# Feed-forwards of a two-block transformer kernel: gate and up weights asked for ahead of the down rows, and a chunk's activations turned behind the first block product of the next chunk

## The reference

```python
def swiglu(h, w_gate, w_up, w_down):
    return (jax.nn.silu(h @ w_gate) * (h @ w_up)) @ w_down

for l in range(DEPTH):                       # DEPTH = 2
    ...
    h = rmsnorm_2(x, norm_pre[l, 0]) * (1.0 + sc1) + sh1
    y = swiglu(h, ffn_w_gate[l, 0], ffn_w_up[l, 0], ffn_w_down[l, 0])
    ...
    h = rmsnorm_2(x, norm_pre[l, 2]) * (1.0 + sc3) + sh3
    y = swiglu(h, ffn_w_gate[l, 1], ffn_w_up[l, 1], ffn_w_down[l, 1])
```

## Time and profile before

| | us |
|---|---|
| three runs | 4084.64, 4093.05, 4095.47; median 4093.05 |
| the profiled execution, device time | 4084.79 |
| its span in the trace | 4083.0 (1.8 lie around it) |
| TensorE busy in the span | 3566.2 (87%) |
| VectorE busy | 2672.0 (65%) |
| ScalarE busy | 701.1 (17%) |
| mean granted TensorE clock | 0.941 of full speed |

### The profile page before, as it was taken

How to read it: one execution, slowest core, us unless ns; L and a number is a source line. 1 busy time by engine, 2 the same in 40 slices (tenths; PEclk the granted TensorE clock), 3 DMA queues, 4 the chain that set the end, 5 groups by cost and what they waited for, 6 DMA issues and landing times. The chain is left out here.

```text
span 4083.0 us, 41858 instructions
## 1 busy us (share of the span) xinstructions
PE 3566.2 (87%) x14754; PEld 2593.6 (64%) x14754; DVE 2672.0 (65%) x5286; ACT 701.1 (17%) x1904; POOL 607.6 (15%) x520
## 2 busy tenths in 40 slices
PE   7999986799998889998997767665889999999999
PEld 3678874677777778776784323222667676667676
DVE  2654778978787767766548887776574543574533
ACT  2531111400000000005212111101001301001301
POOL 0000000033232222210004445442000000000000
PEclk9999998999999999999999988767999999999999
DMA  4466545699999999982658999998883345683353
GB/s 173 154 176 199 148 147 209 205 392 416 412 407 375 399 412 417 417 328 89 181 179 356 416 420 388 422 422 319 276 268 123 134 155 168 229 280 129 125 164 114
DMA packets 486873, 1096.66 MB, mean 269 GB/s; under 512 B 21748, under 2 KB 335092, under 8 KB 419862
## 3 DMA queue, kind: packets, MB, share of 16 engines
q1 hardware_dynamic: 375544, 503.78, 36.4%
q0 software_dynamic: 73728, 536.90, 32.0%
q10 hardware_dynamic: 37408, 53.48, 3.9%
HBM read 1078.36 MB, written 15.73 MB: 268 GB/s over the span
## 5 line engine op out<-in xcount | busy, mean ns | idle before, releaser
L1699 PE MATMUL ps<-hT,wring 128*128 128x256 f32 x2048 | 488.4, 393 | 66.7 <-DMA wring<-in_v_tab 54.2
L1699 PEld LDWEIGHTS ps<-hT,wring 128*128 128x128 f32 x2048 | 395.4, 196 | 152.3 <-issue 87.9
L1690 PE MATMUL ps<-hT,wring 128*128 128x256 f32 x2048 | 470.3, 383 | 1.4 <-ACT G L1759 1.1
L1690 PEld LDWEIGHTS ps<-hT,wring 128*128 128x128 f32 x2048 | 382.9, 190 | 78.4 <-DMA wring<-in_u_first 28.2
L2043 PE MATMUL ps<-pairs,diag 128*128 128x512 f32 x520 | 286.8, 712 | 134.7 <-ACT diag L2138 134.7
L1737 POOL DMA_INDIRECT first_pairs<-in_uv_first_rows,eid x171 | 196.5, 1149 | 1152.5 <-POOLq L135 619.3
L2615 PE MATMUL ps<-wring,hff 128*128 128x512 f32 x704 | 309.4, 592 | 1.7 <-ACT hff L2848 1.7
L2043 PEld LDWEIGHTS ps<-pairs,diag 128*128 128x128 f32 x520 | 116.1, 230 | 303.4 <-ACT diag L2138 164.4
L2576 PE MATMUL ps<-wring,hT 128*128 128x256 f32 x1280 | 302.3, 390 | 0.4 <-DVE xT L3039 0.3
L2100 POOL DMA_INDIRECT pairs<-in_uv_second,eid x172 | 206.4, 1200 | 492.0 <-DVE eid L1339 276.9
L2576 PEld LDWEIGHTS ps<-wring,hT 128*128 128x128 f32 x1280 | 248.2, 197 | 36.3 <-DVE xT L3039 2.4
(11 more groups left out here) (413 smaller groups left out, 5285.8 us busy)
## 6 DMA issues: line engine op xcount, KB each, us to landing
wring<-in_u_first SPq DMA_DIRECT2D x128, 512.0 KB, 14.6
wring<-in_v_tab SPq DMA_DIRECT2D x128, 512.0 KB, 11.2
room<-in_ada_w ACTq DMA_DIRECT2D x32, 1536.0 KB, 10.0
wring<-in_ffn_w_gate SPq DMA_DIRECT2D x44, 1024.0 KB, 7.7
wring<-in_ffn_w_up SPq DMA_DIRECT2D x44, 1024.0 KB, 10.8
wring<-in_ffn_w_down SPq DMA_DIRECT2D x44, 1024.0 KB, 5.0
wring<-in_w_in SPq DMA_DIRECT2D x72, 512.0 KB, 6.6
wring<-in_w_mod SPq DMA_DIRECT2D x28, 1024.0 KB, 5.6
```

The source lines that it names most:

```text
L1690: m = nc.tensor.matmul(ps[:, 4 + e % 2, 0:S], uslot[:, e % 3, k, :], hT[:, k, S:2 * S], start=k == 0, stop=k == KD - 1)
L1699: m = nc.tensor.matmul(ps[:, n // 2, (n % 2) * S:(n % 2 + 1) * S], vslot[:, e % 2, n * P:(n + 1) * P], act_[:, e % 3, :], start=e == 0 and ...
```

## The change

SyncE's list: for chunks 2 to 10 the gate and up transfers of a chunk now stand ahead of the down rows of the chunk before it. TensorE's list: `turn_hidden` of chunk j - 1 no longer stands behind the down product of chunk j - 2, but behind the first of the seven block products of chunk j; that first product, which writes bank 4 anew, gets a wait for the first `Silu` of chunk j - 1, which reads bank 4. The last chunk's `turn_hidden` stays behind its down product. VectorE's and ScalarE's lists are as before.

```diff
                 def load_ffn(F):
...
-                    for j in range(NCH):
+
+                    def gate_and_up(j):
                         s = ffn_slot(F, j)
                         if j >= 2:
                             sp.wait_ge(gu.sem, 2 * NCH * F + 2 * (j - 1))
...
+
+                    def down_rows(j):
+                        s = ffn_slot(F, j)
                         if j >= 2:
                             sp.wait_ge(down.sem, (NCH - 1) * F + j - 1)
...
+
+                    for j in range(2):
+                        gate_and_up(j)
+                        down_rows(j)
+                    for j in range(2, NCH):
+                        gate_and_up(j)
+                        if j > 2:
+                            down_rows(j - 1)
+                    down_rows(NCH - 1)
...
                         pe.wait_ge(combd.sem, 4 * (F + 1))
+                    else:
+                        pe.wait_ge(silu.sem, 2 * NCH * F + 2 * j - 1)
                     pe.wait_ge(wgu[s].sem, 32 * nth(F, j))
                     product(4, lambda k: hT[:, k, 0:P], lambda k: low[:, k, :], True).then_inc(prods.sem, 1)
+                    if j > 1:
+                        turn_hidden(F, j - 1)
...
                     for j in range(1, NCH):
                         split_gate_up(F, j)
                         down_(F, j - 1)
-                        turn_hidden(F, j)
+                    turn_hidden(F, NCH - 1)
```

## The result

The changed kernel takes 4034.14 us (median of 4 runs, 4032.63 to 4038.51) against 4092.1 for the kernel before (4 runs, 4084.64 to 4095.47): a ratio of 0.9863, 95% interval 0.9845 to 0.9880, 58 us less. The profiled execution of the changed kernel took 4033.65 us, its span is 4031.9.

The account below looks back on a forecast made before the run. F = 1 and 3 were taken as bound by TensorE, F = 0 and 2 as losing 58.8 us to late weights (39.9 waits, 18.9 lower clock); 4093.05 less 58.8, no cost added, gave 4034 us, range 4019 to 4060.

Parts of the forecast that it names:

- the 58.8 us of the stages: Chunks 2 to 9 of F = 0 and 2: their loss against F = 1 and 3, 58.8 us, about all to win.
- The moved ask: SyncE: gate and up of the next chunk asked for at T - 6.8 in place of T + 0.2.
- The landing: Gate and up weights: 16.5 us after the ask, 18.0 for a slow one; assumed to land before T + 8.
- T + 8: T is the start of a chunk's first product; at T + 8.0 VectorE wants the next chunk's weights.
- the next wait: TensorE's sixth product waiting for `took` behind VectorE's late sums: 0.65 us a chunk if every landing takes 18.0.
- The moved turning: TensorE: `hidtok` needed at T + 21.1 in place of T + 18.95, so no wait is left ahead of the turning.
- Its cover: Two products, 3.45 us, between turning and fourth product hide the 1.30 us to the end of the copy into `hff`.
- The DMA engines do not become the bound: Rival: queues not kept full, say 300 GB/s, 168 us per eight chunks, 4060; with late landings, 4045 to 4062, chance 0.11.
- The share above 0.95: Sign in the trace after: DMA share above 0.95.
- No change: Rival: transfers sustain only 272 to 280 GB/s, eight chunks stay at 182 us, time 4089; chance 0.06.
- Slower: Rival: chain turning, copy, fourth product over 3.9 us makes all 36 chunks wait; 4110 at 6 us; chance 0.04.
- The clock: TensorE in F = 0 and 2: clock falls to 1.2 GHz after each gap, 18.9 of the 58.8 us.

Follow-up runs that it names:

- e1: Changed kernel with the turning put back behind the down product, only the asks moved: 4032.24 us (4 runs), ratio 0.9863.
- e2: Changed kernel with the asks back in their old order, only the turning moved: 4089.09 us (10 runs), ratio 1.0005.
- e6: Changed kernel with GpSimd also asking for 5 x 0.39 MB of unused rows beside each of chunks 2 to 9, F = 0 and 2: 4034.86 us.
- e7: Changed kernel with the turning behind the third product in place of the first: 4069.79 us (6 runs), ratio to before 0.9953.
- e8: Changed kernel with the turning behind the second product in place of the first: 4031.83 us (1 run).
- e4: Kernel before with seven of eight VectorE modulation sums cut to 8 of 384 columns, output not the reference's: 4089.76 us (1 run).

## Why the prediction was right

The forecast was 4034 us with 4019 to 4060 as its range; the measured median is 4034.14. That the two meet to a fifth of a microsecond is luck. The forecast started from 4093.05, the median of three runs of before; the later 13 and 8 runs have medians of 4086.82 and 4087.05, from which the same sum gives 4028. The runs of the changed kernel spread over 5.9 us, and e1 lies 54.6 us under its 13 runs of before, not 58.8. What was worked out, and came true, is the 58.8 us of the stages and the way to it.

**The bound and the sum.** F = 1 and 3 as the mark for F = 0 and 2 gave 58.8 us; the eight-chunk stretches fell by 30.04 + 28.79 = 58.8 and the medians by 58.0. In the single profiled executions the span fell by less, 4083.0 to 4031.9 = 51.1 us, where 4024.2 was forecast. The other 7.7 us lie in stages that the change does not touch: the second block's first matmul starts at 2839.47 in place of 2835.35, and the two attention stretches between the feed-forwards take 3.7 us more together (below). They go with the single execution and not with the change: that first matmul starts at 2835.35 to 2844.59 in the four profiles with the asks in their old order, and at 2835.48 to 2843.70 in the six with the moved ones.

**The moved ask** was the cause: it alone gives all (e1), the turning alone nothing (e2). Its size was as forecast: gate and up are asked for 6.7 us ahead of the chunk's first product (2882.65 against 2889.32), VectorE no longer waits for them, and L3070 ends 14.9 us behind the chunk's start, as worked out. The landing was the term with the widest margin: 16.5 to 18 us were allowed for and before T + 8 assumed; up landed 7.9 us behind its issue, at about T + 1.6, before the modulation's parts are even asked for (2891.79, T + 2.5). No run moves gate and up ahead of the down rows without asking earlier; the chunks of before that lay behind a stall, with the old order and an earlier ask, speak for the time and not the order. The prediction named `took` as the next wait, with 0.65 us a chunk at landings of 18.0. In e6 that wait came, 3.46 us over eight chunks of F = 2 with the slower matmuls behind it, 0.43 a chunk. But at the 16.3 us that up takes there (it lands at about T + 10), the prediction's own sum has `took` come in time. The term that it lacks is a modulation part that lands late: it lets the sums follow L3053 without a wait, and in e6 VectorE waited 10.1 us there. In the changed kernel itself no such wait occurs.

**The moved turning** costs nothing and gives nothing here. The prediction counted its later deadline (T + 21.1 in place of T + 18.95) as margin; with L3070 at T + 14.9 there was no need of it. Its cover was judged rightly: 3.45 us for a chain of 1.30, and the wait appears as soon as the cover is gone (e7).

**The rivals.** The DMA engines do not become the bound. The prediction took 332 GB/s, a stretch with a share of 0.99, as the ceiling, and held that the trace agreed; e6 moves 373 over 155 us, so that reading was wrong. The share above 0.95 that was to be seen came out as 0.93 and 0.94 over eight chunks, because in chunk 9 no gate and up are left to ask for. Over chunks 2 to 8 of F = 0 it is 0.97:

```profile
2889.32:3025.07 135.75, 135.75 (x534) 98.50 (x532) 116.30 (x181) 11.71 (x28) 0.00 (x0) 1.00 0.97 325
```

The Trainium skill's sentence that transfers from different engines share the 16 DMA engines ("DMA: Bandwidth & Descriptors", "Issuing engines are not separate DMA queues") holds in e6, where GpSimd's loads make the others' landings longer, from 7.9 to 12.5 and 16.3 us for up. It speaks of which engine asks, not of when. The 358 GB/s from HBM for a core on the same page of the Trainium skill (section "Bandwidth"), which that section also gives as each core's part when both cores of an HBM domain stream, was no limit here: one core moved 373 in e6. The rule on shared engines was no obstacle since the change needed no more bytes in a chunk's time, only their spreading over it.

*No change* would have needed 272 to 280 GB/s as what the transfers sustain; the mean was low because the DMA engines rested between bursts, as the prediction had it. *Slower* would have needed a chain from turning to fourth product of more than 3.9 us; e8 puts it under 2.2.

**The clock.** The prediction took 18.9 of the 58.8 us as the lower clock behind each gap. The trace of before shows it in the stretch right behind the gap of chunk 2 in F = 0; the third column from the end is the granted clock, at 0.50, the lower of the two levels:

```profile
2908.94:2911.50 2.56, 2.56 (x8) 2.26 (x9) 2.42 (x5) 0.60 (x1) 0.00 (x0) 0.50 1.08 364
```

With the gaps gone the stretches stand at 1.00. TensorE's busy time for the same products fell by 9.16 us in F = 0 and 9.33 in F = 2, 18.5 in all, close to the 18.9; that is some 2.3 us for each of the eight gaps. No kernel here kept the gaps and lost the low clock, so no run measures the two parts one by one.

## What to carry to other kernels

Where two stages do the same arithmetic, lay them beside each other first: the one without waits is the mark for the other, and the difference, lowered clock included, is the prize. Then ask of the transfer that lands late whether its buffer had been free for long, and what its ask stood behind; an in-order queue that also waits for a later event on behalf of something not urgent makes the urgent one late, and moving the ask cost nothing here. A wait that is merely moved past some work (e2) comes back at the next consumer if the engine that is late stays late.

## What the runs showed of the hardware that was not expected

A busy share of 0.99 did not mean that the DMA engines could take no more: they moved 332 GB/s at that share before the change, and 373 GB/s at 1.06 in e6, GpSimd's loads among them.

The attention stretches between the feed-forwards, the same instructions in all kernels, take 145.25 and 145.15 us in the profile of before, 147.30 and 146.77 in that of after, and from 143.86 (e4) to 149.02 (e8) in the others. Some 5 us of a single execution's span can thus come from stages that nobody changed; why was not tested.
